# Attention by feature: values turned in three places a pair, and the decays loaded over group B's keys

## The reference, cut to what matters

```python
qa, ka, va, logf, qb, kb, vb = project(u, w_in, b_forget)
...
c = jnp.cumsum(logf, axis=1)
...
s = jnp.einsum('bqhd,bkhd->bhqk', qi, k).astype(jnp.float32) * ATTN_SCALE
s = s + (ci[..., None] - cT[:, :, None, :])
s = jnp.where((kpos[None, :] <= qpos[:, None])[None, None], s, NEG_INF)
p = jax.nn.softmax(s, axis=-1)
return jnp.einsum('bhqk,bkhd->bqhd', p.astype(v.dtype), v)
```

## Time and profile before

| | |
|---|---|
| median of 3 runs | 1531.41 us (1531.37 to 1531.96) |
| the profiled execution | 1531.29 us |
| its span, first to last instruction | 1529.3 us |
| mean granted clock of TensorE in it | 0.949 of 2.4 GHz |
| busy: TensorE, DVE, ACT, POOL | 93%, 43%, 32%, 19% of the span |
| load of `cb` | 4 times, 1312 KB, 7.1 us to land (median) |
| load of a weight block | 512 KB, 4.0 us to land (median) |

### The profile page before, as it was taken

How to read it: one execution, slowest core, us unless ns; L and a number is a source line. 1 busy time by engine, 2 the same in 40 slices (tenths; PEclk the granted TensorE clock), 3 DMA queues, 4 the chain that set the end, 5 groups by cost and what they waited for, 6 DMA issues and landing times.

```text
span 1529.3 us, 22397 instructions
## 1 busy us (share of the span) xinstructions
PE 1416.3 (93%) x8951; PEld 1323.1 (87%) x8951; DVE 663.3 (43%) x1256; ACT 491.0 (32%) x1061; POOL 286.3 (19%) x422
## 2 busy tenths in 40 slices
PE   5979997999989876889999999999999999999996
PEld 3868886777777755779999999999999999999996
DVE  6237772442343455366523332524243333325155
ACT  6326672454545455233321112121202111121103
POOL 2125561353524234453000000000000000000000
PEclk9989997998989876899999999999999999999998
DMA  7611113201212174600321102021111112020002
GB/s 190 109 44 29 30 49 94 68 29 33 88 40 71 51 214 150 186 0 1 95 58 42 53 31 70 21 77 42 42 42 42 42 42 58 26 69 17 26 0 114
DMA packets 118671, 94.94 MB, mean 62 GB/s; under 512 B 18752, under 2 KB 109728, under 8 KB 118056
## 3 DMA queue, kind: packets, MB, share of 16 engines
q1 hardware_dynamic: 118568, 93.52, 21.1%
HBM read 74.39 MB, written 19.21 MB: 61 GB/s over the span
## 4 chain that ended last, share of the span: by engine, by line
PE 79%; DVE 7%; DMA 5%; issue 3%; POOL 3%; ACT 3%; SPq 1%; DVEq 0%; ACTq 0%; POOLq 0%
PE ps L566 24%; PE ps L567 23%; PE ps L568 23%; PE ps L754 2%; DMA cb<-c_scratch 1%; DVE sx_x L1539 1%; PE ps L720 1%; DMA x_scratch<-xt_out 1%; PE ps L681 1%; DMA out<-outb 1%; DVE ps L1499 1%; DMA out<-raw 1%; DVE oc L1668 1%; POOL root_b L1971 1%; PE ps L766 1%
## 5 line engine op out<-in xcount | busy, mean ns | idle before, releaser
L1764 DVE TENSOR_TENSOR y_res<-y_res,ps 128x384 f32<-128x384 f32 (+1 forms) x264 | 137.4, 521 | 111.5 <-PE ps L568 111.5
L1750 DVE TENSOR_TENSOR gu<-ps,sg 128x384 f32<-128x384 f32 (+1 forms) x66 | 34.6, 524 | 232.6 <-PE ps L568 231.9
L1931 POOL TENSOR_TENSOR pl_x<-sp_x,ph_x 128x512 fp32r<-128x512 f32 (+5 forms) x120 | 104.1, 882 | 167.0 <-ACT sp_x L1164 165.7
L1347 ACT ACTIVATE h_hi<-gu 128x384 fp32r<-128x384 f32 (+1 forms) x66 | 32.9, 498 | 216.5 <-DVE gu L1750 216.5
L1163 ACT ACTIVATE ph_x<-ps,negc 128x512 fp32r<-128x512 f32 (+5 forms) x120 | 62.6, 522 | 93.3 <-PE ps L766 93.1
L1341 ACT ACTIVATE sg<-ps 128x384 f32<-128x384 f32 (+1 forms) x66 | 30.6, 466 | 175.2 <-PE ps L568 175.2
L566 PE MATMUL ps<-f_hi,ff0hi 128*128 128x384 f32 (+1 forms) x264 | 85.9, 325 | 0.0
L566 PE MATMUL ps<-f_hi,ff2hi 128*128 128x384 f32 (+1 forms) x264 | 85.7, 325 | 0.0
L566 PE MATMUL ps<-f_hi,ff1hi 128*128 128x384 f32 (+1 forms) x264 | 85.7, 325 | 0.0
L566 PE MATMUL ps<-f_hi,ff3hi 128*128 128x384 f32 (+1 forms) x264 | 85.7, 325 | 0.0
L567 PE MATMUL ps<-f_lo,ff1hi 128*128 128x384 f32 (+1 forms) x264 | 85.4, 323 | 0.0
(11 more groups left out here) (327 smaller groups left out, 4039.3 us busy)
## 6 DMA issues: line engine op xcount, KB each, us to landing
raw<-in_w_gate SPq DMA_DIRECT2D x22, 512.0 KB, 5.4
raw<-in_w_up SPq DMA_DIRECT2D x22, 512.0 KB, 4.9
raw<-in_w_down SPq DMA_DIRECT2D x22, 512.0 KB, 4.2
raw<-in_w_in SPq DMA_DIRECT2D x14, 512.0 KB, 4.0
cb<-c_scratch SPq DMA_DIRECT2D x4, 1312.0 KB, 7.1
xt<-in_x_prompt SPq DMA_DIRECT2D x8, 512.0 KB, 4.0
out<-outb SPq DMA_DIRECT2D x16, 256.0 KB, 2.7
xin<-in_x_prompt SPq DMA_DIRECT2D x8, 512.0 KB, 4.8
```

The costliest lines, as they stand in the source:

```text
L1347: act.activation(h_hi[par][:, f, c0:c0 + n], gu[(f + c) % 2][:, 0:n], ACT.Copy).then_inc(S["g_hi"], 1)
L1750: dve.tensor_tensor(gu[(f + c) % 2][:, 0:n], bank(3 + c, n), sg[c][:, 0:n], ALU.mult)\
L1764: dve.tensor_tensor(y, y, bank(6 + o % 2, n), ALU.add).then_inc(S["d_y"], 1)
L1931: pool.tensor_tensor(pl_x[at][0:rows, 0:n], sp_x[at][0:rows, 0:n], ph_x[at][0:rows, 0:n].bitcast(F32), ALU.subtract).then_inc(S["x_pl"], 1)
```

## The change

The turns go to the places in VALUES_AT: for pair 0 place -7 part 3, place -6 part 3 and place -5 part 0; for pairs 1 to 3 places 15 i - 2 part 3, 15 i part 3 and 15 i + 1 part 0. ACT's copies wait only for the values that read the same blocks in the pair before, and the products of units 0, 8 and 12 wait for the turn that brings their blocks. `cb` now lies over group B's keys, the first load of it is issued at s = 17, when all window scores and the values of window 15 are done; the buffers that lay there move over group B's values, and the first exponential waits for the stores of the windows' outputs.

```diff
+VALUES_AT = [(0, 2 - LEAD, 3, (0, 4)), (0, 3 - LEAD, 3, (4, 4)), (0, 4 - LEAD, 0, (8, 1))]
+for _i in range(1, PAIRS):
+    VALUES_AT += [(_i, NFU * _i - 2, 3, (0, 4)), (_i, NFU * _i, 3, (4, 4)), (_i, NFU * _i + 1, 0, (8, 1))]
...
+        for i_, at_, part_, a_ in VALUES_AT:
+            if at_ == v and part_ == 0:
+                task(("x", v, part_), "fv", i_, *a_)
         if v == 3 - LEAD:
-            for a in ((0, 4), (4, 4), (8, 1)):
-                task(("x", v, 0), "fv", 0, *a)
             pending += turns[6:9]
...
+        for i_, at_, part_, a_ in VALUES_AT:
+            if at_ == v and part_ == 3:
+                task(("x", v, part_), "fv", i_, *a_)
         if j == 3 and 0 <= v < NX:
             task(("x", v, 4), "amx", i, 1)
-        if j == 0 and 0 < v < NX:
-            for a in ((0, 4), (4, 4), (8, 1)):
-                task(("x", v, 4), "fv", i, *a)
...
-        (cb, am_x0, am_x1), end = lay(qk_end, ("cb", [P, 2, CW_WIDTH], F32), ("am_x0", [P, TOK], F32R), ("am_x1", [P, TOK], F32R))
-        am_x = (am_x0, am_x1)
+        (am_x0, am_x1, ph_x3, ot_x, sx_x), end = lay(
+            qk_end, ("am_x0", [P, TOK], F32R), ("am_x1", [P, TOK], F32R), ("ph_x3", [P, 512], F32R), ("ot_x", [P, 512], F32), ("sx_x", [P, 512], F32))
+        assert end <= qk_end + 2 * 10 * 3 * HD * 4
+        (cb,), end = lay(qk_end + 2 * 10 * 3 * HD * 4, ("cb", [P, 2, CW_WIDTH], F32))
...
-                if j == 0:
-                    pe.wait_ge(S["ev_act"], act_done(T_OF["fv", i, 8, 1]))
-                    pe.wait_ge(S["ev_dve"], dve_done(T_OF["fv", i, 8, 1]))
+                for unit, a in ((0, (0, 4)), (8, (4, 4)), (12, (8, 1))):
+                    if j == unit:
+                        pe.wait_ge(S["ev_act"], act_done(T_OF["fv", i, *a]))
+                        pe.wait_ge(S["ev_dve"], dve_done(T_OF["fv", i, *a]))
...
-                    if t0 == 0:
-                        if i == 0:
-                            act.wait_ge(S["w_pv"], 2 * NWU)
-                            act.wait_ge(S["w_ttr"], 4 * NWU)
-                        else:
-                            act.wait_ge(S["x_pv"], 2 * NFU * i)
+                    if i >= 1:
+                        act.wait_ge(S["x_pv"], 2 * (NFU * (i - 1) + {0: 8, 4: 12, 8: NFU}[t0]))
+                    elif t0 == 0:
+                        act.wait_ge(S["w_pv"], 2 * NWU)
+                        act.wait_ge(S["w_ttr"], 4 * NWU)
...
+                if v == 0:
+                    act.wait_ge(S["og_w0"], 16 * TILES)
+                    act.wait_ge(S["og_w1"], 16 * TILES)
...
                 else:
-                    sp_.wait_ge(S["w_pv"], 2 * NWU)
+                    sp_.wait_ge(S["w_s"], 2 * WB0[NWU])
+                    sp_.wait_ge(S["w_pv"], 2 * (NWU - 2))
...
                 if s >= 2:
                     store_window(s - 2)
-            load_decays(0)
+                if s == NWU - 1:
+                    load_decays(0)
             store_window(NWU - 1)
```

More of the change, by code:

```diff
@@ L442, in build @@
             qw_lo.append(lo)
-        (cb, am_x0, am_x1), end = lay(qk_end, ("cb", [P, 2, CW_WIDTH], F32), ("am_x0", [P, TOK], F32R), ("am_x1", [P, TOK], F32R))
-        am_x = (am_x0, am_x1)
+        (am_x0, am_x1, ph_x3, ot_x, sx_x), end = lay(
+            qk_end, ("am_x0", [P, TOK], F32R), ("am_x1", [P, TOK], F32R), ("ph_x3", [P, 512], F32R), ("ot_x", [P, 512], F32), ("sx_x", [P, 512], F32))
+        assert end <= qk_end + 2 * 10 * 3 * HD * 4
+        (cb,), end = lay(qk_end + 2 * 10 * 3 * HD * 4, ("cb", [P, 2, CW_WIDTH], F32))
         sp_x, end = lay(end, *many("sp_x", 4, [P, 512], F32))
-        (ph_x3, ot_x, sx_x), end = lay(end, ("ph_x3", [P, 512], F32R), ("ot_x", [P, 512], F32), ("sx_x", [P, 512], F32))
-        ph_x = (*ph_parts, ph_x3)
+        am_x, ph_x = (am_x0, am_x1), (*ph_parts, ph_x3)
         assert end <= common
```

## The result

The changed kernel takes 1519.54 us (median of five runs, 1515.26 to 1521.42) against 1531.37 us (1527.14 to 1531.96) before, in runs on the same chip: a ratio of 0.9926 [0.9905, 0.9948]. That is 11.3 us less by the ratio (0.0074 of 1531.4), 8 to 15 us by its interval. The prediction was 5.2 us less and ended its range at 1520.5. The profiled execution took 1521.21 us.

What follows compares the result with a forecast made beforehand. TensorE, busy for 93% of the span, bounds the kernel, so its idle time and clock can move the end. Terms −3.9 − 1.6 + 9.0 − 7.2 − 1.5 = −5.2 us gave 1526.1 us, range 1520.5 to 1531.5.

Steps and rivals of the forecast that it cites:

- Edit 1: Pair 0's first minima: earlier `cb` load removes TensorE's 2.28 us wait and the slow stretch behind; −3.9 us, at worst −2.3.
- Edit 2: Pair 0's value turns, spread out: the store's wait is hidden, two shorter waits remain; −1.6 us (−4.2 to +0.8).
- Edit 3: Two units before pairs 0 to 2 end: first turn waits behind the RECIPROCAL, delaying minima 8; +3.0 us each, +9.0.
- Edit 4: Boundaries after pairs 0 to 2: last values to minima 10 shorten by 2.4 us each, clock another 0.5 each.
- The edits costed at nothing: Waits by block at the values, the new buffer layout, the first exponential's wait for window stores: no cost.
- Rival 1: Pair ends: new turn behind the RECIPROCAL costs 4.2 us each, boundary minima gain only 1 each; 1535.4 us, chance 0.10.
- Rival 2: Pair 0 and later pairs: slow clock stretches reappear behind the new waits and pay everything back; 1530.2 us, chance 0.22.
- Rival 3: Clock stays up: pair 0's turns give −4.2 us, the pairs −2.5 in sum; 1520.7 us, chance 0.12.
- Rival 4: First minima: `cb` arrives no earlier, held by its waits or the queue; 1530 us, chance 0.06.

Runs made afterwards that it cites:

- the part alone: The kernel before with only the earlier `cb` load and what belongs to it: 1519.19 us, ratio 0.9946 to before.
- e2: The kernel before with only pair 0's turns at their new places: 1528.02 us, ratio 1.0004 to before.
- e3: The kernel before with only the turns of pairs 1 to 3 at their new places: 1525.75 us, ratio 0.9988 to before.
- the change again: The changed kernel measured once more, nothing altered: 1520.41 us, ratio 0.9943 to before.
- c1: The kernel before with only the second chunk's RECIPROCAL and multiply one place later on DVE in pairs 0 to 2: 1512.56 us, ratio 0.9878 to before.

## Why the prediction was wrong in its size

- **Edit 1, predicted −3.9, at worst −2.3: this is the step that failed.** Distance A fell by 6.1 us against the very execution that was read, and the part alone gave 8.2 (5 to 11) on the whole time. The prediction took the 2.28 us of idle that one execution showed as the length of the wait, and with it the low clock ahead of the wait (0.67 over 5.35 us of work) as a property of the program. In the trace of the change that work takes 3.1 us at full clock (238.92 to 241.98), so 2.2 us more came out; with them the term would have been −6.1. For the clock that it had read the term was right: the two traces of changed kernels whose clock was low there are 3.6 us below that execution. But only 3 of the 14 traces have that clock. Its last part held: minima 1 to 2 take 2.62 us after and were forecast at 4.1 − 1.6. Of the 8.2 us, the some 2 beyond A lie within what two executions of one kernel differ by later on; no run settles them.
- **Edit 2, predicted −1.6 (−4.2 to +0.8).** The mechanism is as forecast: two waits of 2.10 and 3.36 us (2.6 and 3.6 forecast), ACT's key copy standing for the third turn. B fell by 3.0 in this trace and by 0.2 in e2; e2's time says +0.6 (−1.8 to +3.1). The bounds held, the choice of the middle was as good as any.
- **Edit 3, predicted +3.0 a pair.** Minima 7 to 8 grew by 3.1, 2.9 and 3.1 us. Right. The four transposes took 0.60 us where nothing had slowed the clock, and 0.90 to 1.11 behind the wait. The Trainium skill's figure (TensorE: Matmul & The Clock Gate, Part 4, PE-mode transpose) of about 275 ns for one agrees with the trace: at full clock each of the four at 433.45 lasts 270 to 273 ns. But they start 0.11 us apart and overlap, so the estimate that adds four of them up, 1.1 us, does not hold at full clock.
- **Edit 4, predicted −2.9 a pair with the clock.** From minima 8 to 11 the kernel took 4.0, 3.1 and 3.2 us less, 0.2 to 1.1 more than forecast. The pairs together: −1.3 by C, −1.8 [−4.1, +0.3] in e3, +0.3 forecast: the draw that the prediction called it.
- **The edits costed at nothing** cost nothing that can be seen: no wait at the values' own line for a turn, none of the first exponential for the stores.
- **The rivals.** Rival 1 named the place that mattered most, the turn behind the RECIPROCAL, but gave the boundary a gain of 1 us a pair, and it gained 3.1 to 4.0, which paid for the shift. What neither it nor the prediction asked is what the RECIPROCAL cost before the change. Rival 2 (the clock takes it back) doesn't hold for edit 1: in the profiled execution the clock stayed at 1.00 up to 250.3, and where it fell (the change again, A of 8.09) 3.7 us of the gain against before were left. Rival 3 came nearest in time (1520.7). By the ruler 3.0 of the 5 us beyond the forecast lie where it had them, in pair 0's turns and the pairs, but the runs of the parts do not bear that out: they give edit 1 4.3 us more than forecast, edit 2 2.2 less and the pairs 2.1 more, with intervals of 2 to 3 us either way. Rival 4 is refuted: `cb` was issued at 231.81.

The sum in the trace, by the ruler: +0.6 ahead of minima 0, −6.1 (edit 1), −3.0 (edit 2), −1.3 (pairs), −0.4 in the rest: −10.2, the span's difference. 2.2 of the 5 us that were missing are edit 1's, 1.4 are edit 2's and 1.6 the pairs'. The last two are no more than such a kernel's executions differ by; the first is the clock at one place, read from one execution and taken as fixed. That the time fell 1 us below the range has some luck in it, too: measured again, the change gained 8.7 us, which the range takes in.

## What to carry to other kernels

A wait for something that arrives at a time of its own is as long as from the end of the work ahead, at full clock, to that arrival; if the stretch ahead of it ran at a low clock, the idle that the profile prints is shorter by what the low clock took, and is the right price only if the clock is low there after the change as well. So before pricing such a wait, compare the clock ahead of it between two executions. And look at what each engine's long instruction stands in front of: a RECIPROCAL of 3.35 us, needed by nobody soon, stood in front of a reduction that TensorE needed at once, and moving it behind that reduction gave more than a new plan for the values.

## What the runs showed of the hardware

- The granted clock at one place of the program isn't fixed by the program: ahead of minima 0 it was 0.60 in one execution of the kernel before and 1.00 in the other; distance A was 5.68 and 8.09 us in two executions of the change, C 204.3 and 209.5.
- Idle stretches of 3.4, 1.9 and 2.0 us ahead of minima 8 cost 4.5, 3.6 and 3.6 us, read from what came out when they went (c1): the products behind them ran at a granted clock of 0.50 to 0.72, and at 1.00 where the idle was gone.
- Taking these three waits away (7.3 us of idle, of which 1.4 came back at mx (1, 9)) took 18.7 us off the time (14.6 to 22.8); by the ruler 15.6 us of it lie in C, and no run settles where the rest, if it is any, comes from.
